# Softmax layers by pairs of heads on VectorE and ScalarE; the sparse layer's selection and splits in a new order

## The chip, the cores and the metric

The program runs on one core of a Trainium2 chip. The metric is device time in microseconds (us). The kernel before took 989.56 us (median of 3 runs, 987.58 to 989.96). Engines: PE is TensorE (PEld its weight loads), DVE VectorE, ACT ScalarE, POOL GpSimd, SP SyncE, which issues the weight loads from HBM.

## The reference

Two blocks run on 256 tokens of 1024 features, in fp32. The first has four layers: short convolution, sparse attention, latent attention, short convolution. The second has a pooling and a stick-breaking attention layer. The change touches the sparse and the latent layer.

```python
def dsa_mixer(xn, ...):      # sparse: 16 heads of 64, index 8 heads of 64
    q, k, v, z, qi, ki, wi = jnp.split(xn @ w_in, cuts, axis=-1)
    q = rope(rmsnorm(q, q_norm), positions); k = rope(rmsnorm(k, k_norm), positions)
    # score = sum over index heads of wi * relu(qi . ki), hidden keys masked
    # the 64 (seq // 4) largest scores of each query are kept
    # o = softmax(q k^T / 8 over the kept keys) v
    return (o * silu(z)) @ w_out

def mla_mixer(xn, ...):      # latent: 16 heads of 96 (64 + 32 rotary), v of 64
    cq, ckv, kr, z = jnp.split(xn @ w_in, cuts, axis=-1)
    q = (rmsnorm(cq, ..) @ w_uq); kv = (rmsnorm(ckv, ..) @ w_ukv)   # then norms, rope
    o = dense_chunk_attention(q, k, v, C_QK ** -0.5)
    return (o * silu(z)) @ w_out
```

## The kernel before

**Numbers in two parts.** Weights come in as fp32 (`raw`). ACT copies them to a shorter float (`whi`), DVE subtracts that from `raw` and leaves the low part (`wlo`). Activations are split alike (`xh`, `xl`, and `yh`, `yl` for gated outputs). `three` multiplies high by high, low by high and high by low, so a product costs three matmuls.

**Units.** Weights are streamed in units of 128 rows by 4096 columns, numbered B0, B0+1, ... for the sparse and C0, C0+1, ... for the latent layer. A unit stands in buffer u % 2 of `raw`, `whi` and `wlo`, so two are in flight. A split is done in halves of 2048 columns (`split`, DVE L883, ACT L470) or quarters of 1024 (`split_quarter`, DVE L902, ACT L478). In both loops of heads the out projection's last unit has its quarters' subtraction on POOL (L1581). Semaphores `landed`, `hi_ready`, `lo_ready`, `unit_done` connect SP, ACT, DVE and PE.

**Order.** Nothing schedules: each engine's instruction list is written out by hand, in the functions marked by engine, and an instruction waits on semaphores for its operands. So the order on each queue is the order of the code.

**Sparse layer.** B0 holds the index queries, B0+1 the index key and weights (`wi`), B0+2 to B0+5 the halves of q and k in turn (L396). For each of B0 and B0+2 to B0+5 (e = 0 to 4) ACT copies the accumulator (`token_raw`) and squares it (`token_squares`), DVE sums, DVE and ACT make the norm's factor (`half_mean`, `half_root`, `half_factor`), DVE and POOL apply norm and rotary (`token_turn`, `token_rope`), PE transposes (`turn_tokens`) and ACT or DVE copies the transposes (`token_out`). `index_scores` makes the eight heads' scores, ACT takes their relu, DVE sums them (`index_head`). `top64` selects: one pass that hides masked keys, then eight rounds of MAX (the 8 largest) and MATCH_REPLACE (which marks them), and a compare into `pick`. It is called for the first 128 queries (128 keys) and for the others (256 keys). B0+6 and B0+8 are the two halves of v, B0+7 and B0+9 those of z, B0+10 and B0+11 the out projection.

**Loops of heads.** `softmax_heads` runs on DVE and ACT for each layer. DVE reduces the logits of a head to a row minimum (L1171), ACT takes two exponentials (L669, L671), DVE divides by the sum (L1180, L1182), PE transposes, ACT copies the transposes (L678), PE multiplies with v, DVE multiplies by the gate (L1150). PE runs `paired_heads`: logits, transposes and products of two heads per step, between them one *filler* f: part of B0+8 or B0+9 (C0+7) or of the out projection (`attention_out`, a *piece*). ACT switches its function table for silu and back (`preload_act_table_set`). Behind the loop `attention_last_out` does the rest of the out projection. Before, DVE and ACT take one head a step (18 steps).

## Time and profile before

| | |
|---|---|
| runs | 989.56 us median, 987.58 to 989.96 |
| profiled execution | 994.89 us, its span 993.3 us, mean granted clock 0.97 |
| busy shares | PE 93%, PEld 87%, DVE 65%, ACT 50%, POOL 32% |
| sparse layer's token units, its loop, its rest | 131.2 to 235.2, to 308.1, to 325.4 us |
| latent layer's loop | 387.8 to 452.1 us |

The profile is of one execution. A granted clock of 1 is 2.4 GHz for TensorE, 0.5 is 1.2 GHz; a stretch's number is the mean over it. Idle time of an engine that PE does not wait for costs nothing.

### The profile page before, as it was taken

What the parts mean: (1) busy time and instruction counts of PE and PEld (TensorE: products, weight loads), DVE (VectorE), ACT (ScalarE), POOL (GpSimd) and SP (SyncE); (2) the same over time, 40 slices, a digit from 0 to 9 for tenths busy, and PEclk for the clock granted to TensorE, in tenths of its full rate; (3) what the DMA queues carried; (4) which work ended last, traced back from release to release, by engine and by line L of the source; (5) the groups of instructions that cost most, each with busy time, mean ns of one, the idle gap of its engine ahead of it and who ended that gap; (6) DMA issues with size and microseconds to landing.
All of it is one profiled execution on the core that took longest, in us unless ns stands there. A gap on an engine that the chain in (4) does not pass through costs nothing.

```text
span 993.3 us, 16780 instructions
## 1 busy us (share of the span) xinstructions
PE 924.2 (93%) x6761; PEld 865.9 (87%) x6761; DVE 643.1 (65%) x1005; ACT 500.3 (50%) x710; POOL 317.4 (32%) x270
## 2 busy tenths in 40 slices
PE   6999989988889996979999999899999999999986
PEld 5999978667668985869999999799999997988986
DVE  5776665895574788765576667587656554656642
ACT  5544454444574677673453352434445336575631
POOL 8433223343013225112543326955302000123320
PEclk9999999998889999799999999899999999999999
DMA  9876344434114425225477443344654562334401
GB/s 250 224 203 207 127 170 170 138 117 170 47 42 146 165 65 190 93 59 147 130 205 219 169 171 127 129 171 169 253 181 160 199 215 104 136 119 162 172 28 43
DMA packets 123585, 148.70 MB, mean 150 GB/s; under 512 B 9561, under 2 KB 79102, under 8 KB 123518
## 3 DMA queue, kind: packets, MB, share of 16 engines
q1 hardware_dynamic: 121472, 145.63, 45.3%
q0 software_dynamic: 464, 1.02, 0.4%
q10 hardware_dynamic: 1582, 1.12, 0.4%
q8 instruction: 47, 0.77, 0.3%
q14 instruction: 20, 0.16, 0.1%
HBM read 146.70 MB, written 1.05 MB: 149 GB/s over the span
## 4 chain that ended last, share of the span: by engine, by line
PE 61%; DVE 8%; ACT 7%; POOL 3%; issue 2%; ACTq 0%; DVEq 0%; POOLq 0%
PE acc L1652 43%; PE aux L1652 16%; DVE wlo L883 2%; POOL arena L1507 1%; POOL arena L1508 1%; ACT whi L478 1%; ACT arena L504 1%; ACT work L671 1%; POOL arena L1506 1%; ACT whi L470 1%; DVE score L1126 1%; PE aux L1996 1%; DVE arena L985 1%; DVE top L1125 1%; ACT work L678 1%
## 5 line engine op out<-in xcount | busy, mean ns | idle before, releaser
L883 DVE TENSOR_TENSOR wlo<-raw,whi 128x2048 fp32r<-128x2048 f32 (+5 forms) x118 | 281.0, 2408 | 104.9 <-ACT whi L470 103.1
L1652 PE MATMUL acc<-xh,whi 128*128 128x256 f32 x1128 | 323.9, 287 | 4.9 <-DVE wlo L883 4.2
L1652 PE MATMUL acc<-xl,whi 128*128 128x256 f32 x1128 | 321.1, 285 | 0.0
L1652 PE MATMUL acc<-xh,wlo 128*128 128x256 f32 x1128 | 321.0, 285 | 0.0
L470 ACT ACTIVATE whi<-raw 128x2048 fp32r<-128x2048 f32 (+5 forms) x118 | 202.9, 1748 | 85.1 <-PE aux L1652 44.0
L1652 PEld LDWEIGHTS acc<-xh,whi 128*128 128x128 f32 x1128 | 218.4, 194 | 6.8 <-issue 5.8
L1652 PEld LDWEIGHTS acc<-xl,whi 128*128 128x128 f32 x1128 | 218.3, 193 | 0.0
L1652 PEld LDWEIGHTS acc<-xh,wlo 128*128 128x128 f32 x1128 | 218.0, 193 | 0.0
L1652 PE MATMUL acc<-whi,xh 128*128 128x512 f32 (+1 forms) x208 | 83.4, 401 | 7.9 <-DVE arena L985 4.0
L1571 POOL CAST yh<-ytmp 128x256 fp32r<-128x256 f32 x24 | 17.0, 706 | 220.4 <-DVE ytmp L1409 123.3
L1652 PE MATMUL aux<-yh,whi 128*128 128x256 f32 x288 | 81.9, 284 | 0.0
L1652 PE MATMUL aux<-yh,wlo 128*128 128x256 f32 x288 | 81.5, 283 | 0.0
L1652 PE MATMUL aux<-yl,whi 128*128 128x256 f32 x288 | 81.5, 283 | 0.0
L1652 PE MATMUL acc<-whi,xl 128*128 128x512 f32 (+1 forms) x208 | 80.5, 387 | 0.0
L1652 PE MATMUL acc<-wlo,xh 128*128 128x512 f32 (+1 forms) x208 | 80.5, 387 | 0.0
L1652 PEld LDWEIGHTS acc<-whi,xh 128*128 128x128 f32 x208 | 40.2, 193 | 18.8 <-issue 6.5
L1652 PEld LDWEIGHTS aux<-yh,whi 128*128 128x128 f32 x288 | 55.3, 192 | 0.3 <-issue 0.3
L902 DVE TENSOR_TENSOR wlo<-raw,whi 128x1024 fp32r<-128x1024 f32 x44 | 53.9, 1225 | 2.2 <-ACT whi L478 2.2
L1652 PEld LDWEIGHTS aux<-yl,whi 128*128 128x128 f32 x288 | 55.3, 192 | 0.0
L1652 PEld LDWEIGHTS aux<-yh,wlo 128*128 128x128 f32 x288 | 55.3, 192 | 0.0
L1506 POOL TENSOR_TENSOR arena<-arena 128x1024 f32<-128x1024 f32 x5 | 12.1, 2412 | 124.5 <-ACT arena L504 124.5
L478 ACT ACTIVATE whi<-raw 128x1024 fp32r<-128x1024 f32 x48 | 50.1, 1046 | 0.0
(341 smaller groups left out, 1763.0 us busy)
## 6 DMA issues: line engine op xcount, KB each, us to landing
raw<-in_a_w_in SPq DMA_DIRECT2D x52, 512.0 KB, 6.6
raw<-in_sb_w_in SPq DMA_DIRECT2D x48, 512.0 KB, 5.5
raw<-in_b_w_in SPq DMA_DIRECT2D x36, 512.0 KB, 5.5
raw<-in_pool_w_in SPq DMA_DIRECT2D x32, 512.0 KB, 5.6
raw<-in_a_w_out SPq DMA_DIRECT2D x16, 512.0 KB, 5.0
raw<-in_pool_w_out SPq DMA_DIRECT2D x16, 512.0 KB, 5.0
raw<-in_sb_w_out SPq DMA_DIRECT2D x16, 512.0 KB, 4.9
raw<-in_b_w_out SPq DMA_DIRECT2D x8, 512.0 KB, 4.7
```

The costliest lines, as they stand in the source:

```text
L470: A(whi[b][:, lo:hi], (raw_third if third else raw[b])[:, lo:hi], ACT.Copy).then_inc(hi_ready, 1)
L478: ins = A(whi[u % 2][:, c * q:c * q + c], raw[u % 2][:, c * q:c * q + c], ACT.Copy)
L504: A(arena[:, 4 * n:4 * n + 4, :], xT[:, 4 * n:4 * n + 4, :], ACT.Square)\
L671: A(L[:, P:W384], L[:, P:W384], ACT.Exp, bias=st[:, 1:2], scale=nf[:, HEADS + i:HEADS + i + 1], accum_out=st[:, 3:4]).then_inc(sem("exp_re ...
L678: A(work[:, 2 + h % 2, :], aux[:, 2 + h % 2, 0:W384], ACT.Copy)\
L883: TT(wlo[b][:, lo:hi], (raw_third if third else raw[b])[:, lo:hi], whi[b][:, lo:hi].bitcast(F32), ALU.subtract).then_inc(lo_ready, 1)
L902: ins = TT(wlo[u % 2][:, c], raw[u % 2][:, c], whi[u % 2][:, c].bitcast(F32), ALU.subtract)
L985: ins = TT(dst, src, rb, ALU.mult)
L1125: me.link(V.max(top8[:, :], s))
L1506: me.link(TT(arena[:, 0:4, :], arena[:, 0:4, :], arena[:, 4:8, :], ALU.add))
L1571: nc.gpsimd.tensor_copy(hi, ytmp[:, :]).then_inc(sem("yh_ready"), 1)
L1652: return nc.tensor.matmul(out_, lhsT, rhs, start=start, stop=stop, skip_group_check=True)
```

## The change

- `softmax_heads` on DVE and ACT goes by pairs: two minima, the splits' quarters, two divisions (DVE); two heads' exponentials, two copies, two quarters (ACT), in eight steps and a tail.
- All quarters are subtracted on DVE, POOL's four of each loop go. The quarters' steps move; C0+7, which was split whole ahead of the latent loop, becomes quarters inside it, and is PE's filler 3, 5, 6, 8 there (before 5, 6, 8, 9). B0+9 is filler 5, 6, 8, 9 (before 6 to 9).
- Two more pieces of the out projection (half 1 of two tiles) become fillers 15 and 16, and `attention_last_out` has two fewer.
- `silu` of B0+7's z moves behind the first two heads' exponentials. The latent loop's turned heads 12 to 15 are spread over fillers 0 and 2.
- B0+2's first half is split in two quarters ahead of the layer's norm factor; the scores of the eight index heads stand in B0+3's steps 1 to 7 and B0+4's first, before in B0+4's eight; the token turns move one unit ahead.
- `top64` becomes `hide`, `take_largest(rounds)` and `chosen`: of the first 128 queries' eight rounds 3, 2 and 3 stand between the splits of B0+5, of the others' eight 3 ahead of B0+7's split and 5 behind it.

Lines that were removed, added or moved, with "..." where some are left out:

```diff
-        SPARSE_SPLITS = {first + q: (u, q) for first, u in ((2, B0 + 9), (8, B0 + 10), (12, B0 + 11)) for q in range(4)}
-        MLA_SPLITS = {first + q: (u, q) for first, u in ((2, C0 + 8), (11, C0 + 9)) for q in range(4)}
+        def quarters(u, halves):
+            return {step: tuple((u, 2 * half + n) for n in range(2)) for half, step in enumerate(halves)}
+        SPARSE_SPLITS = {**quarters(B0 + 9, (0, 1)), **quarters(B0 + 10, (3, 4)), **quarters(B0 + 11, (6, 7))}
+        MLA_SPLITS = {**quarters(C0 + 7, (0, 1)), **quarters(C0 + 8, (3, 4)), **quarters(C0 + 9, (6, 7))}
...
+            nc.scalar.preload_act_table_set("natural_log_exp_and_others")
             renorm(1, G_B)
             split(B0 + 1)
-            root(1)
-            nc.scalar.preload_act_table_set("natural_log_exp_and_others")
+            def first_half(u):
+                act.wait_ge(landed[u % 2], 64 * (u // 2))
+                act.wait_ge(unit_done, u - 1)
+                for q in range(2):
+                    c = slice(1024 * q, 1024 * q + 1024)
+                    A(whi[u % 2][:, c], raw[u % 2][:, c], ACT.Copy).then_inc(hi_ready if q else sem("quarter_hi"), 1)
+            first_half(B0 + 2)
+            root(1, log=True)
...
-            split(B0 + 2, (0,))
+            split(B0 + 2, (1,))
             act.wait_ge(sem("rt_ready"), 2)
             token_raw(0)
-            split(B0 + 2, (1,))
             act.wait_ge(unit_done, B0 + 2)
...
-            token_raw(1)
-            split(B0 + 4, (0,))
             act.wait_ge(sem("ki_turned"), 1)
             A(arena[:, 36, :], aux[:, 0, 0:T], ACT.Copy).then_inc(sem("ki_out"), 1)
             token_out(0)
-            token_squares(1)
-            split(B0 + 4, (1,))
-            token_raw(2)
+            token_raw(1)
             for h in range(8):
                 act.wait_ge(sem("idx_s"), h + 1)
...
                 if h == 1:
-                    split(B0 + 5, (0,))
-                if h == 3:
-                    token_squares(2)
-                if h == 5:
-                    split(B0 + 5, (1,))
+                    split(B0 + 4, (0,))
+                if h == 2:
+                    token_squares(1)
+                if h == 4:
+                    split(B0 + 4, (1,))
+            token_raw(2)
+            split(B0 + 5, (0,))
+            token_squares(2)
+            token_out(1)
+            split(B0 + 5, (1,))
             half_root(0)
             token_raw(3)
             split(B0 + 6, (0,))
             token_squares(3)
-            token_out(1)
+            token_out(2)
             split(B0 + 6, (1,))
             token_raw(4)
             split(B0 + 7, (0,))
             token_squares(4)
-            token_out(2)
             split(B0 + 7, (1,))
+            token_out(3)
             half_root(1)
-            token_out(3)
-            split(B0 + 8)
+            split(B0 + 8, (0,))
...
             values(vB, B0 + 6, 0, 0)
+            split(B0 + 8, (1,))
+            token_out(4)
...
-            silu(24, 4, 1)
             def softmax_heads(layer):
-                nc.scalar.preload_act_table_set("natural_log_exp_and_others")
                 h0 = HEADS * layer
                 y_count[0] += 8
-                for i in range(HEADS + 2):
-                    if layer == 0 and i == 4:
+                for j in range(HEADS // 2 + 1):
+                    for i in (2 * j, 2 * j + 1):
+                        if i < HEADS:
...
+                    if layer == 0 and j == 0:
+                        silu(24, 4, 1)
+                        nc.scalar.preload_act_table_set("natural_log_exp_and_others")
+                    if layer == 0 and j == 2:
                         values(vB, B0 + 8, 1, 1)
...
-                    if layer == 0 and i == 11:
-                        silu(28, 4, 2)
-                        nc.scalar.preload_act_table_set("natural_log_exp_and_others")
...
+                    if layer == 1 and j < 2:
+                        turn_copy(12 + 2 * j)
+                    if j:
+                        for h in (2 * j - 2, 2 * j - 1):
+                            act.wait_ge(sem("pt_psum"), h0 + h + 1)
+                            if h >= 2:
+                                act.wait_ge(sem("pv_done"), h0 + h - 1)
...
+                    for u, q in (SPARSE_SPLITS, MLA_SPLITS)[layer].get(j, ()):
+                        split_quarter(u, q)
+                    if j == 5:
+                        silu(44 if layer else 28, 4, 4 if layer else 2)
                         nc.scalar.preload_act_table_set("natural_log_exp_and_others")
...
+            def first_half(u):
+                for q in range(2):
+                    c = slice(1024 * q, 1024 * q + 1024)
+                    if q == 0:
+                        dve.wait_ge(sem("quarter_hi"), 1)
+                    else:
+                        dve.wait_ge(hi_ready, 2 * u + 1)
+                    TT(wlo[u % 2][:, c], raw[u % 2][:, c], whi[u % 2][:, c].bitcast(F32), ALU.subtract)\
+                        .then_inc(lo_ready if q else sem("quarter_lo"), 1)
+            mean_square(1)
+            first_half(B0 + 2)
...
+            newton(rT[:, 4:6], rT[:, 0:2], rT[:, 6:8]).then_inc(sem("rt_ready"), 1)
...
+            def hide(lo, hi):
                 s = score[:, lo:hi]
                 me.link(STT(s, mask[:, lo:hi], HIDDEN / NEG, s, ALU.mult, ALU.add))
-                for _ in range(TOPK // 8):
+            def take_largest(lo, hi, rounds):
+                s = score[:, lo:hi]
+                for _ in range(rounds):
...
-                TS(pick[:, lo:hi], s, (HIDDEN + TAKEN) / 2, NEG, ALU.is_gt, ALU.mult).then_inc(sem("picked"), 1)
+            def chosen(lo, hi):
+                TS(pick[:, lo:hi], score[:, lo:hi], (HIDDEN + TAKEN) / 2, NEG, ALU.is_gt, ALU.mult).then_inc(sem("picked"), 1)
+            for h in range(8):
+                index_head(h)
+                if h == 2:
+                    split(B0 + 4, (0,))
+                if h == 4:
+                    token_sums(1)
+                if h == 5:
+                    split(B0 + 4, (1,))
             dve.wait_ge(sem("mask_in"), 16)
-            top64(0, P)
+            hide(0, P)
+            take_largest(0, P, 3)
+            token_turn(2)
+            split(B0 + 5, (0,))
+            token_sums(2)
+            half_mean(0)
+            take_largest(0, P, 2)
+            half_factor(0)
+            split(B0 + 5, (1,))
+            take_largest(0, P, 3)
+            chosen(0, P)
+            token_turn(3)
             split(B0 + 6, (0,))
-            token_turn(3)
             token_sums(3)
             split(B0 + 6, (1,))
-            top64(P, W384)
+            hide(P, W384)
+            take_largest(P, W384, 3)
+            token_turn(4)
             split(B0 + 7, (0,))
-            token_turn(4)
             token_sums(4)
             half_mean(1)
             split(B0 + 7, (1,))
             half_factor(1)
+            take_largest(P, W384, 5)
+            chosen(P, W384)
             split(B0 + 8)
             take(B0 + 7, 24, "z_raw")
+            dve.wait_ge(sem("picked"), 2)
...
-            split(C0 + 7)
...
+                splits = (SPARSE_SPLITS, MLA_SPLITS)[layer]
+                def minima(i):
...
+                def division(h):
...
+                for j in range(HEADS // 2 + 2):
+                    if j == 5:
+                        take(C0 + 7 if layer else B0 + 9, 44 if layer else 28, "z_raw")
+                    if j < HEADS // 2:
+                        minima(2 * j)
+                        minima(2 * j + 1)
+                    if layer == 1 and j < 2:
+                        turn_copy(13 + 2 * j)
+                    if j >= 2:
+                        t = j - 2
...
+                    for n in range(2):
+                        if j - 1 in splits:
+                            split_quarter(*splits[j - 1][n])
+                        if j < HEADS // 2:
+                            division(2 * j + n)
...
-            def attention_low(u):
+            def attention_low():
                 for t in range(NK):
                     y_parts(yh[:, t, :], yl[:, t, :])
-                    if t in (4, 5):
...
-                        TT(wlo[u % 2][:, c], raw[u % 2][:, c], whi[u % 2][:, c].bitcast(F32), ALU.subtract)\
-                            .then_inc(lo_ready if t == 5 else sem("low_quarter"), 1)
...
+                    if u == B0 + 2 and k in (0, 2):
+                        pe.wait_ge(lo_ready if k else sem("quarter_lo"), 2 * u + 1 if k else 1)
+                    elif k in (0, 4):
...
+            def index_first(k):
+                if k:
+                    index_scores(k - 1)
+            def index_last(k):
+                if k == 0:
+                    index_scores(7)
+                if k == 3:
+                    turn_tokens(1)
...
-            token_unit(B0 + 3, ki_turn)
+            token_unit(B0 + 3, index_first)
             taken("tok_raw", 4)
-            token_unit(B0 + 4, index_scores)
+            token_unit(B0 + 4, index_last)
             taken("tok_raw", 6)
-            token_unit(B0 + 5, turn_at({2: 1}))
+            token_unit(B0 + 5, turn_at({5: 2}))
             taken("tok_raw", 8)
-            token_unit(B0 + 6, turn_at({4: 2}))
+            token_unit(B0 + 6, turn_at({4: 3}))
             taken("tok_raw", 10)
-            unit(B0 + 7, in_tiles(1), xh, xl, turn_at({4: 3}))
+            unit(B0 + 7, in_tiles(1), xh, xl, turn_at({6: 4}))
...
-                if 6 <= f < 10:
-                    if f == 6:
+                if f in (5, 6, 8, 9):
+                    if f == 5:
                         taken("v_ready", 4)
-                    unit(B0 + 9, in_tiles(1), xh, xl, part=(2 * (f - 6), 2))
-                if f in (12, 13, 15, 16):
-                    if f == 12:
-                        taken("z_raw", 2)
-                    attention_out(B0 + 10, 8, (12, 13, 15, 16).index(f), 0)
+                    unit(B0 + 9, in_tiles(1), xh, xl, part=(2 * (5, 6, 8, 9).index(f), 2))
+                out_filler(f, 0)
+            def out_filler(f, layer):
+                u, y0 = (C0 + 8, 16) if layer else (B0 + 10, 8)
+                if f == 11:
+                    taken("z_raw", 2 * layer + 2)
+                if 11 <= f < 15:
+                    attention_out(u, y0, f - 11, 0)
+                if 15 <= f < 17:
+                    if f == 15:
+                        taken("logits", HEADS * layer + HEADS)
+                    attention_out(u, y0, f - 15, 1)
...
-                if f < 2:
-                    turn_heads(12 + 2 * f)
-                    turn_heads(13 + 2 * f)
-                if f in (5, 6, 8, 9):
-                    if f == 5:
-                        taken("turn_out_v", 7)
+                if f in (0, 2):
+                    turn_heads(12 + f)
+                    turn_heads(13 + f)
+                if f in (3, 5, 6, 8):
+                    if f == 3:
+                        taken("turn_out_v", 8)
                         taken("turn_out_a", 8)
-                    unit(C0 + 7, in_tiles(1), xh, xl, part=(2 * (5, 6, 8, 9).index(f), 2))
-                if f in (12, 13, 15, 16):
-                    if f == 12:
-                        taken("z_raw", 4)
-                    attention_out(C0 + 8, 16, (12, 13, 15, 16).index(f), 0)
+                    unit(C0 + 7, in_tiles(1), xh, xl, part=(2 * (3, 5, 6, 8).index(f), 2))
+                out_filler(f, 1)
...
-                for k in range(4):
+                for k in range(2, 4):
```

**DVE, ahead of B0+7's split.** In the rows below `raw_50`, `whi_52` and `wlo_54` are the buffers of odd units, `raw_49`, `whi_51`, `wlo_53` those of even ones. Before:

```order
L1125 MAX top_115<-score 128x8
L1126 MATCH_REPLACE score<-top_115,score 128x256
L1127 TENSOR_SCALAR pick<-score 128x256
L883 TENSOR_TENSOR wlo_54<-raw_50,whi_52 128x2048
L1054 TENSOR_TENSOR sqy<-sqy,qk_tab 128x8x32
L1055 TENSOR_TENSOR sqy<-sqy,qk_tab 128x8x32
```

The same place in the changed kernel:

```order
L1145 MAX top_115<-score 128x8
L1146 MATCH_REPLACE score<-top_115,score 128x256
L1082 TENSOR_TENSOR sqy<-sqy,qk_tab 128x8x32
L1083 TENSOR_TENSOR sqy<-sqy,qk_tab 128x8x32
L1082 TENSOR_TENSOR sqy<-sqy,qk_tab 128x8x32
L1083 TENSOR_TENSOR sqy<-sqy,qk_tab 128x8x32
L892 TENSOR_TENSOR wlo_54<-raw_50,whi_52 128x2048
L1091 TENSOR_REDUCE hf<-sqy 128x8 x2
L1096 TENSOR_SCALAR hf<-hf 128x4x8
L892 TENSOR_TENSOR wlo_54<-raw_50,whi_52 128x2048
```

Before, the eighth round and the pick stand right ahead of the first half. Now the third round does, with the last token turn between; five rounds and the pick follow the second half.

**ACT, start of the sparse loop.** L646 (L659) writes v, L653 (L668) is silu, L586 (L600) a copy of transposes. Before:

```order
L470 ACTIVATE whi_51<-raw_49 128x2048 x2
L646 ACTIVATE vB<-acc,rT 128x512 x2
L653 ACT_TABLE_LOAD
L653 ACTIVATE arena<-arena 128x1024
L658 ACT_TABLE_LOAD
L669 ACTIVATE work,stat<-work,stat,nf 128x128
L671 ACTIVATE work,stat<-work,stat,nf 128x256
L669 ACTIVATE work,stat<-work,stat,nf 128x128
L671 ACTIVATE work,stat<-work,stat,nf 128x256
L586 ACTIVATE arena<-acc 128x4x128 x2
```

After:

```order
L474 ACTIVATE whi_51<-raw_49 128x2048
L659 ACTIVATE vB<-acc,rT 128x512 x2
L474 ACTIVATE whi_51<-raw_49 128x2048
L600 ACTIVATE arena<-aux 128x4x128 x2
L679 ACTIVATE work,stat<-work,stat,nf 128x128
L681 ACTIVATE work,stat<-work,stat,nf 128x256
L679 ACTIVATE work,stat<-work,stat,nf 128x128
L681 ACTIVATE work,stat<-work,stat,nf 128x256
L668 ACT_TABLE_LOAD
L668 ACTIVATE arena<-arena 128x1024
L685 ACT_TABLE_LOAD
L482 ACTIVATE whi_52<-raw_50 128x1024 x2
```

The values stand between B0+8's halves, and silu with its two table loads behind the first two heads.

**ACT, start of the latent loop.** L709 (L719) copies turned heads. Before:

```order
L709 ACTIVATE arena<-acc,G 96x512
L470 ACTIVATE whi_52<-raw_50 128x2048 x2
L658 ACT_TABLE_LOAD
L669 ACTIVATE work,stat<-work,stat,nf 128x128
L671 ACTIVATE work,stat<-work,stat,nf 128x256
L709 ACTIVATE arena<-acc,G 96x512
```

After:

```order
L719 ACTIVATE arena<-acc,G 96x512
L679 ACTIVATE work,stat<-work,stat,nf 128x128
L681 ACTIVATE work,stat<-work,stat,nf 128x256
L679 ACTIVATE work,stat<-work,stat,nf 128x128
L681 ACTIVATE work,stat<-work,stat,nf 128x256
L719 ACTIVATE arena<-acc,G 96x512
L482 ACTIVATE whi_52<-raw_50 128x1024 x2
```

C0+7's split (two halves of 2048) is gone from ahead of the exponentials and follows as quarters.

## Rows read from the trace of the kernel before

**Rows 1.** The page's first part: each engine's busy time.

```profile
PE 924.2 (93%) x6761; PEld 865.9 (87%) x6761; DVE 643.1 (65%) x1005; ACT 500.3 (50%) x710; POOL 317.4 (32%) x270
```

**Rows 2.** Stretches: us, busy PE, PEld, DVE, ACT, POOL, clock, DMA, GB/s.

```profile
131.20:235.20 104.00, 96.58 (x486) 78.71 (x484) 77.92 (x141) 53.31 (x70) 42.87 (x36) 0.97 0.43 151
235.20:308.10 72.90, 59.73 (x378) 47.74 (x377) 43.20 (x150) 44.85 (x102) 10.82 (x15) 0.84 0.22 77
308.10:325.40 17.30, 17.30 (x147) 17.24 (x144) 7.01 (x10) 5.27 (x8) 2.99 (x5) 1.00 0.57 193
387.80:452.10 64.30, 51.31 (x337) 42.19 (x336) 47.07 (x153) 42.01 (x97) 13.30 (x18) 0.87 0.23 67
```

**Rows 3.** PEld's timeline: start, us, instruction, [idle before, releaser].

```profile
148.75 0.19 PEld L1652 LDWEIGHTS acc<-whi,xh 128*128 128x128 f32 x1 [3.48 <-issue]
...
221.53 0.29 PEld L1652 LDWEIGHTS acc<-xh,whi 128*128 128x128 f32 x1 [4.56 <-issue]
...
238.79 0.29 PEld L1652 LDWEIGHTS acc<-whi,xh 128*128 128x128 f32 x1 [2.92 <-DVE arena L985]
...
397.06 0.66 PEld L1953 LDWEIGHTS acc<-cst,qraw 128*96 128x96 f32 x4 [6.53 <-ACT arena L709]
```

**Rows 4.** Stretches at either clock, columns as in rows 2.

```profile
131.10:141.90 10.80, 10.80 (x50) 8.97 (x49) 6.16 (x7) 4.76 (x7) 6.61 (x12) 1.00 0.37 123
273.10:281.40 8.30, 8.30 (x72) 7.47 (x70) 3.65 (x17) 4.22 (x12) 1.13 (x2) 1.00 0.29 118
411.00:416.90 5.90, 5.90 (x48) 5.20 (x48) 4.49 (x18) 1.58 (x5) 1.13 (x2) 1.00 0.01 3
221.50:228.50 7.00, 6.94 (x47) 6.97 (x48) 6.74 (x13) 0.46 (x2) 2.74 (x2) 0.79 0.02 1
238.70:247.00 8.30, 8.21 (x24) 6.48 (x24) 2.18 (x14) 4.57 (x10) 0.00 (x0) 0.63 0.64 248
```

**Rows 5.** ACT's timeline ahead of B0+2.

```profile
144.39 1.91 ACT L470 ACTIVATE whi<-raw 128x2048 fp32r<-128x2048 f32 x1
146.21 1.25 ACT L571 ACTIVATE sqy<-acc,rT 128x512 f32<-128x512 f32 x2
```

**Rows 6.** DVE's timeline at the selection's end and at B0+8.

```profile
211.05 0.43 DVE L1125 MAX8 top<-score 128x8 f32<-128x256 f32 x1
...
219.13 2.28 DVE L883 TENSOR_TENSOR wlo<-raw,whi 128x2048 fp32r<-128x2048 f32 x1
...
232.19 5.34 DVE L883 TENSOR_TENSOR wlo<-raw,whi 128x2048 fp32r<-128x2048 f32 x2 [3.78 <-ACT whi L470]
```

**Rows 7.** DVE's timeline: one head of the sparse loop.

```profile
263.03 0.28 DVE L1171 CUSTOM_DVE_ANT_0 work<-aux,pick 128x128 f32<-128x128 f32 x1
...
263.78 0.16 DVE L1180 RECIPROCAL stat<-stat 128x2 f32<-128x2 f32 x1
...
264.44 1.22 DVE L902 TENSOR_TENSOR wlo<-raw,whi 128x1024 fp32r<-128x1024 f32 x1
```

**Rows 8.** ACT's timeline: one head of the sparse loop.

```profile
291.91 1.28 ACT L684 ACT_TABLE_LOAD   x1
293.21 0.49 ACT L669 ACTIVATE work<-work,stat,nf 128x128 f32<-128x128 f32 x1
...
294.29 0.47 ACT L678 ACTIVATE work<-aux 128x384 f32<-128x384 f32 x1
294.66 1.04 ACT L478 ACTIVATE whi<-raw 128x1024 fp32r<-128x1024 f32 x1
```

**Rows 9.** ACT's groups, 235.2 to 308.1: busy, mean ns, idle before.

```profile
L646 ACT ACTIVATE vB<-acc,rT 128x512 f32<-128x512 f32 x2 | 1.3, 684 | 0.0
```

**Rows 10.** ACT's timeline, start of the latent loop.

```profile
396.34 0.67 ACT L709 ACTIVATE arena<-acc,G 96x512 f32<-96x512 f32 x1
```

**Rows 11.** Timelines of DVE and of POOL, end of the latent loop.

```profile
447.19 3.03 DVE L1182 TENSOR_SCALAR work<-work,stat 128x128 f32<-128x128 f32 x2
...
447.70 2.37 POOL L1581 TENSOR_TENSOR wlo<-raw,whi 128x1024 fp32r<-128x1024 f32 x1
```

127 lines of the change are left out of this document (37 added, 90 removed).

## The prediction

> **What bounds the kernel now.** I read the page first: TensorE (PE) is busy 93% of the span [rows 1], so the change can only win where PE waits or runs at its low clock. Then the table of stretches over the layers that the diff touches [rows 2]. The reader is to see four things in it. In the token projections (131.2 to 235.2) PE is busy 96.6 of 104.0 us. In the sparse layer's softmax loop (235.2 to 308.1) it is busy 59.7 of 72.9 us, and the granted clock is 0.84. In the output part behind it (308.1 to 325.4) it never waits: 144 matmuls in 17.3 us, 0.12 each. In the latent layer's loop (387.8 to 452.1) it is busy 51.3 of 64.3 us at clock 0.87. Then PE's timeline shows where the long waits are [rows 3]: 3.5 us ahead of unit B0+2, 4.6 ahead of B0+7, 2.9 ahead of B0+8, and 6.5 in the latent layer, where the turned heads wait for ScalarE (ACT). Last, stretches at either clock give the prices [rows 4]: B0's 48 matmuls of 512 columns take 10.8 us (0.225 each) at 2.4 GHz, but 24 of them take 8.2 (0.34) behind the 2.9 us wait; B0+7's first 47 of 256 columns take 7.0 instead of 5.6 behind the 4.6 us wait. A wait of 3 to 5 us thus costs another 1.3 to 2.7 us of low clock.
>
> Two undisturbed stretches give the cost of one pair of heads. 273.1 to 281.4 holds a pair and 48 filler matmuls (5.8 us), so the pair costs 2.5; 411.0 to 416.9 holds a pair of the latent layer and 24 fillers (2.9), so 3.0.
>
> **Start of B0+2.** PE needs the two accumulator copies of B0 (token_raw) and the first low part. Before, ACT does a half split (1.9), then the copies, which start at 146.21 and end at 147.5 [rows 5]; VectorE (DVE) then subtracts until 148.6. Now ACT does two quarters from 142.1, two small logarithm steps, the other half, then the copies: 142.1 + 1.9 + 0.5 + 1.9 + 1.1 = 147.6. DVE's first quarters are ready by 145.4. So the copies end it and not the split: 1.1 us gained of 3.5. Bounds: nothing, and 3.5 plus the low clock behind it, 1.5. I take 1.1, since every term of it is a copy whose row exists. The table switches that the diff takes away here lie ahead of the copies.
>
> **Index scores and turns moved.** The eight index steps keep their number and their switches of array shape; they only start seven steps earlier. Token turns 0 and 1 move ahead of B0+5, 2 to 4 each one unit ahead; five are then done when the loop begins, instead of four. That puts one turn, 1.0 us, ahead of the loop and takes it out of it. Nothing queued behind them becomes late by my walk: relu h is 0.5 us, and DVE's step with a split behind it ends before the next but one.
>
> **The selection's rounds spread.** Eight rounds on 256 columns and a pick of 0.2 stand between 211.05 and 219.13 [rows 6], 0.98 a round. They are one piece ahead of B0+7's first half (219.13, 2.28 us), which PE waits for until 221.5. Now three rounds stand ahead of it and five behind its second half. The half moves 5 rounds earlier against its surroundings (4.9 us), and PE's need does not move: B0+6 ends near 217.4, the half is ready near 214.8, the second near 218.4 against a need of 223. The wait of 4.6 and the low clock's 1.3 go. What is late next is B0+8: the rounds end near 224.6, both halves near 229.1, and `take` (1.2) waits for B0+7's end near 229.9. The walk's slack is 2.6, 4.6 and 0.8 us; if DVE were 1 us later throughout, only the last would cost. Before, that place was held by ACT, which came to B0+8 late: DVE idled 3.8 us for it [rows 6].
>
> Sum to the loop's start: 1.1 + 4.6 + 1.3 - 1.0 (the fifth turn) = 6.0 us.
>
> **The sparse loop.** Before: 8 pairs 20.0, B0+8 10.8, B0+9's 96 matmuls 11.5, four output pieces 5.8, one turn 1.0: 49.1 us of work in 72.9, so 23.8 lost. Now two more output pieces (half 1, 24 matmuls, 2.9 us) fill it, and the turn is gone: 51.0. For the waits I walked the four queues pair by pair. Prices: minima 0.75 and division 0.66 a head, a quarter 1.14 on DVE [rows 7]; exponentials 1.08 a head on ACT (293.21 to 294.29), a copy 0.4 and a quarter 1.0 [rows 8], so DVE's fullest step is 2 x (0.75 + 0.66 + 1.14) + 0.4 for the gate = 5.5 us and ACT's 2 x (1.08 + 0.4 + 1.0) = 5.0, against 5.4 to 8.3 on PE with two fillers. Because each split quarter now stands between a minimum and the division that waits for ACT, DVE has something to do in that gap. Waits that remain: 0.9 for B0+7's `take`; 2.7 at filler 5, where the second value half comes behind two minima, two heads' exponentials and 1.3 us of copies [rows 9] (0.75 + 2.2 + 1.3 + 0.2 = 4.4 after the logits, of which PE fills 1.7), with 1.5 of low clock behind it; 0.9 at the last pair. That is 6.0. For waits too short for such a walk I add 0.5 a pair, 4.0. Loop: 61.0, gain 11.9 us. Bounds: 0 (every wait only moves) and 21.9 (none is left). Behind the loop 24 matmuls fewer: 2.9 us, sure, since that stretch has no waits [rows 2].
>
> **The latent loop.** Before: 8 x 3.0, C0+7 11.5, four pieces 5.8, four turned heads 1.8: 43.1 of 64.3, 21.2 lost. The 6.5 us wait came from C0+7's whole split ahead of the loop: two halves of 2.28 on DVE [rows 6], and ACT's turn copy (0.67) only after the first exponentials, at 396.34 [rows 10]. Now the loop starts at once, but C0+7 becomes filler 3, and its first two quarters come late on DVE: four minima 3.0, two turn copies 1.4 (like ACT's), three divisions 2.0, five small factor steps of 0.2 each, like the reciprocal, 1.0, two quarters 2.3: 9.8 us after the first logits, while PE has 4.7 of work. So 5.2 us of that wait come back, with 2.5 of low clock, and 0.9 at the end: 8.6, and 4.0 as above. 46.0 + 8.6 + 4.0 = 58.6, gain 5.7. Bounds: 0 and 18.3. Again 2.9 behind the loop.
>
> **POOL gives up its four low quarters.** While it did them, two divisions on DVE (0.66 a pair normally) took 3.0 us [rows 11]. DVE pays 1.14 for each instead. The gain is inside the walk (the last pairs).
>
> The SBUF page of the Trainium skill ("SBUF — State Buffer", Who interferes with whom) says that a VectorE operation with two SBUF inputs and a GpSimd operation that reads SBUF exclude one another for the whole instruction. It makes a rival, below.
>
> ACT's table loads take 1.28 us and the exponential starts 0.02 later [rows 8]; the loops keep six of them. The Trainium skill ("ScalarE: Activation LUTs", What ACT_TABLE_LOAD costs) gives 2.66 us for a switch, with a drain behind the load. By that the two switches at step 5 of each loop would delay the exponentials by 2.8 us more, and the sum would be near 966; by the row there is no drain here, and I leave it out.
>
> **Sum.** 6.0 + 11.9 + 2.9 + 5.7 + 2.9 = 29.4 us. The profiled execution took 994.89 (span 993.3), so it would take 965.5; the median of the runs is 989.56, 5.3 lower, and I take the same difference off it: 960.2 us.
>
> **Rivals.**
> (a) The pairs hand over one at a time: ACT's copies wait for transposes behind a filler, and its splits stand behind the copies, so PE waits once a pair. For it: in the old latent loop PE waited 6.5 us for one copy of ACT that stood behind other work [rows 3, 10]. Against: PE's fillers last longer than either chain. Half of the loops' gain goes: 8.8 us, 969.
> (b) The exclusion above: the last token's product on GpSimd (rope) now ends near 224.1, DVE's B0+8 split begins near 224.6. If GpSimd is 0.5 us late, two subtractions of 2.28 [rows 6] pass ahead of it, PE waits some 2.5 us in B0+7 and runs low behind it: 5 us, 965. For it: [rows 11] show one engine stretched beside the other. Against: the slack, though small.
> (c) Slower: PE's short waits in both loops keep it at 1.2 GHz. Its work there, 97 us, costs 1.5 times as much at that level [rows 4], 48.5 us. It eats the gain from 60% of the loops' work on; at four fifths it costs 38.8, and the time is 970 + 29 = 999. Against: the clock of the old loops is 0.84 and 0.87, with more waits.
> (d) Next to nothing left: filler 3 and filler 5 find their operands in time: 950.
> (e) The change does not reach the path: the same time. Only if every removed wait reappears; the 5.8 us of output work moved into waits speak against it.
>
> **Numbers.** The forecast 0.70 (own range 952 to 968), (a) 0.13, (b) 0.05, (c) 0.04, (d) 0.05, (e) 0.03. Range 948 to 975. 0.3%, 3 us, is about what a measurement of this kernel can tell from no change: faster 0.93, same 0.03, slower 0.04.
>
> **What would show it.** No wait ahead of B0+7; B0+2 starting 2.3 to 2.5 us after B0+1; B0+8 starting 7 to 9 us earlier; loop B 58 to 64 us and loop C 56 to 62; one wait of about 3 us at filler 5 and one of about 5 ahead of C0+7; 120 matmuls in 14.4 us behind each loop; no DVE division of 3 us. I am wrong if the loops take over 68 and 62 us, or if their clock falls under 0.8.

## The result and the profile after

The changed kernel takes 965.67 us (median of 4 runs, 965.41 to 966.42) against 989.55 (987.58 to 989.96). The ratio is 0.9747, with a 95% interval of 0.972 to 0.9775, so it is 23.9 us faster. The forecast was 960.2, with a range of 948 to 975. One run of the kernel before, beside the experiments, took 1132.9 us at a clock of 0.749 and is left out of every comparison.

Its profiled execution took 965.70, with a span of 964.1. I read the page's first part first, as in [rows 1].

```profile
PE 907.5 (94%) x6761; PEld 853.6 (89%) x6761; DVE 651.7 (68%) x1011; ACT 498.3 (52%) x712; POOL 322.0 (33%) x266
```

PE's instructions are as many as before, yet it is busy 16.7 us less. Nothing was taken out of its work; the same matmuls ran at a higher clock. The table of stretches, with the columns of [rows 2], shows where: the token units, the sparse loop, its tail, the latent loop and its tail.

```profile
131.80:234.70 102.90, 95.64 (x495) 77.09 (x493) 83.81 (x141) 52.53 (x71) 45.02 (x36) 1.00 0.44 152
234.70:294.50 59.80, 53.20 (x393) 43.88 (x392) 45.41 (x152) 43.81 (x100) 12.59 (x14) 0.97 0.27 94
294.50:309.10 14.60, 14.60 (x124) 14.49 (x121) 7.33 (x11) 5.28 (x8) 1.14 (x2) 1.00 0.71 234
371.40:427.00 55.60, 47.77 (x361) 41.45 (x360) 45.77 (x157) 40.46 (x98) 13.27 (x16) 0.97 0.25 76
427.00:441.50 14.50, 14.50 (x123) 14.36 (x120) 8.87 (x11) 6.34 (x8) 1.13 (x2) 1.00 0.76 206
```

The granted clock of the loops rose from 0.84 and 0.87 [rows 2] to 0.97 in both. The next table sets the stages of the two traces side by side. Their bounds are read from PE's timeline: the end of the layer before, the first logits, the last product with v, and the last matmul of the out projection. They add up within 0.1 us, by rounding.

| stage | before | after | gain | forecast |
|---|---|---|---|---|
| start of B0 | 131.2 | 131.9 | -0.7 | 0 |
| B0 to the sparse loop | 104.2 | 102.8 | 1.4 | 6.0 |
| sparse loop | 72.6 | 59.7 | 12.9 | 11.9 |
| its tail | 17.5 | 14.6 | 2.9 | 2.9 |
| up to the latent loop | 62.4 | 62.4 | 0 | 0 |
| latent loop | 64.1 | 55.5 | 8.6 | 5.7 |
| its tail | 17.5 | 14.6 | 2.9 | 2.9 |
| the rest | 523.8 | 522.5 | 1.3 | 0 |
| span | 993.3 | 964.1 | 29.2 | 29.4 |

The sum came out and the stages did not: the token units gave 4.6 us less than forecast, the two loops 3.9 more and the rest 0.6 more. That the sum fits is luck. PE's timeline after, with the columns of [rows 3], has the waits:

```profile
148.43 0.19 PEld L1693 LDWEIGHTS acc<-whi,xh 128*128 128x128 f32 x1 [2.48 <-ACT sqy L585]
...
202.93 0.20 PEld L1860 LDWEIGHTS aux<-cst,sqy 128*128 128x128 f32 x2 [3.06 <-POOL sqy L1608]
...
208.17 0.19 PEld L1693 LDWEIGHTS acc<-whi,xh 128*128 128x128 f32 x1 [0.88 <-issue]
...
221.80 0.19 PEld L1693 LDWEIGHTS acc<-xh,whi 128*128 128x128 f32 x1 [1.99 <-issue]
...
237.04 0.19 PEld L1693 LDWEIGHTS acc<-whi,xh 128*128 128x128 f32 x1 [1.80 <-DVE arena L994]
...
255.19 0.19 PEld L1693 LDWEIGHTS acc<-xh,whi 128*128 128x128 f32 x1 [2.99 <-ACT vB L659]
...
382.78 0.29 PEld L1693 LDWEIGHTS acc<-xh,whi 128*128 128x128 f32 x1 [5.34 <-issue]
```

These are the starts of B0+2, token 2's transposes (in B0+5), B0+6, B0+7, B0+8, B0+9 (filler 5) and C0+7. Ahead of B0+2 and B0+7 the waits shrank from 3.48 and 4.56 [rows 3] to 2.48 and 1.99. The 3.06 and the 0.88 are new. Filler 5 and C0+7 wait as forecast (2.7 and 5.2).

### The profile page after: what moved, and what is told of

Its sections match the earlier page's. It is cut to its first block, busy times and chain, and to the rows that moved or that the text cites. A ratio compares the mean times of both kernels' runs of the same rounds, so it can differ in the third digit from the quotient of the medians.

```text
span 964.1 us, 16784 instructions
## 1 busy us (share of the span) xinstructions
PE 907.5 (94%) x6761; PEld 853.6 (89%) x6761; DVE 651.7 (68%) x1011; ACT 498.3 (52%) x712; POOL 322.0 (33%) x266
## 4 chain that ended last, share of the span: by engine, by line
PE 60%; DVE 10%; ACT 6%; POOL 3%; issue 2%; ACTq 0%; POOLq 0%; DVEq 0%
PE acc L1693 43%; PE aux L1693 16%; DVE wlo L892 3%; POOL arena L1553 1%; ACT work L681 1%; POOL arena L1554 1%; ACT arena L508 1%; POOL arena L1552 1%; ACT work L679 1%; DVE arena L994 1%; DVE score L1146 1%; ACT work L695 1%; DVE sqy L1083 1%; DVE top L1145 1%; DVE work L1209 0%
## 5 line engine op out<-in xcount | busy, mean ns | idle before, releaser
L892 DVE TENSOR_TENSOR wlo<-raw,whi 128x2048 fp32r<-128x2048 f32 (+5 forms) x115 | 276.6, 2432 | 85.7 <-ACT whi L474 83.9
L474 ACT ACTIVATE whi<-raw 128x2048 fp32r<-128x2048 f32 (+5 forms) x115 | 197.3, 1744 | 78.6 <-PE acc L1693 38.1
L1617 POOL CAST yh<-ytmp 128x256 fp32r<-128x256 f32 x24 | 24.3, 1011 | 216.9 <-DVE ytmp L1455 123.3
L911 DVE TENSOR_TENSOR wlo<-raw,whi 128x1024 fp32r<-128x1024 f32 x52 | 64.8, 1250 | 2.0 <-ACT whi L482 1.9
L482 ACT ACTIVATE whi<-raw 128x1024 fp32r<-128x1024 f32 x52 | 53.1, 1048 | 0.0
```

The costliest lines, as they stand in the source:

```text
L474: A(whi[b][:, lo:hi], (raw_third if third else raw[b])[:, lo:hi], ACT.Copy).then_inc(hi_ready, 1)
L482: ins = A(whi[u % 2][:, c * q:c * q + c], raw[u % 2][:, c * q:c * q + c], ACT.Copy)
L892: TT(wlo[b][:, lo:hi], (raw_third if third else raw[b])[:, lo:hi], whi[b][:, lo:hi].bitcast(F32), ALU.subtract).then_inc(lo_ready, 1)
L911: ins = TT(wlo[u % 2][:, c], raw[u % 2][:, c], whi[u % 2][:, c].bitcast(F32), ALU.subtract)
L1617: nc.gpsimd.tensor_copy(hi, ytmp[:, :]).then_inc(sem("yh_ready"), 1)
```

## What stretched in the token units

The wait of 3.06 us is for GpSimd's last product of token 2. POOL's timeline has its two products of that kind, and DVE's timeline two splits and a rotary product in the same stretches:

```profile
195.90 2.95 POOL L1608 TENSOR_TENSOR sqy<-sqy,hf 128x512 f32<-128x512 f32 x1 [6.10 <-DVE nf L1105]
...
201.78 1.10 POOL L1608 TENSOR_TENSOR sqy<-sqy,hf 128x512 f32<-128x512 f32 x1
```

```profile
187.13 1.53 DVE L1083 TENSOR_TENSOR sqy<-sqy,qk_tab 128x256 f32<-128x256 f32 x1
188.58 3.37 DVE L892 TENSOR_TENSOR wlo<-raw,whi 128x2048 fp32r<-128x2048 f32 x1
...
218.32 3.37 DVE L892 TENSOR_TENSOR wlo<-raw,whi 128x2048 fp32r<-128x2048 f32 x1
```

The same product takes 2.95 us beside a split and 1.10 alone. A half split takes 3.37 instead of 2.28 [rows 6], and 218.32 is the half of B0+7 that PE waits for. On the way to token 2's transposes, the rotary product (1.53 instead of 0.42), the split behind it and GpSimd's product come one after the other, and together they take 4.1 us more than alone. That is an estimate from these rows; by it the stretching is enough for the whole wait of 3.06.

This is the exclusion that rival (b) spoke of, in other places. The rule of the Trainium skill ("SBUF — State Buffer", Who interferes with whom), that a VectorE operation with two SBUF inputs and a GpSimd operation that reads SBUF keep each other out, agrees with these rows: the product that starts at 195.90 ends at 198.85, 0.9 us behind the split that began at 195.67 and took 2.28.

## The experiments

The changed kernel was timed once, in the 4 runs above. Before's median beside the later groups of runs was 989.62 (for the first four experiments), 989.97 (the next four) and 991.15 (the last four), so a difference of 1 to 2 us from 965.67 is no more than these groups differ by themselves. A ratio is to before's runs of the same group, with its 95% interval.

Theory: the loops gain by the pairs' order, in place; in the token units PE asks for token 2 earlier than GpSimd can have it, and the splits beside the rotary work are stretched. Rivals: the loops' gain is low clock of one traced execution; VectorE's own queue limits the token units.

**The kernel before once more, traced.** No edit.

> The kernel before, once more with a profile. Its profiled execution took 994.89 us, 5.3 over the median of 989.55, and I had taken that 5.3 as an offset that the changed kernel would have too; it did not (profiled 965.70, median 965.67). Theory: the excess is low clock in the two softmax loops that most executions don't have, so this execution comes to 987 to 990 and its loops are 2 to 5 us shorter than 72.8 and 64.3. Rival: being profiled costs this kernel 5 us; then it takes 994 to 996 with the same loops.

It took 997.70 us. The two loops are as long as in the first trace, to 0.1 us, by PE's timeline; the bounds here are rounded (columns of [rows 2]):

```profile
235.50:308.30 72.80, 59.68 (x378) 47.75 (x376) 43.12 (x150) 44.75 (x102) 10.69 (x15) 0.84 0.22 77
388.00:452.30 64.30, 49.84 (x337) 40.97 (x336) 47.05 (x153) 41.99 (x97) 13.27 (x18) 0.89 0.23 67
```

My forecast for this execution failed, and the loops did not get shorter. The rival asked for 994 to 996 with the same loops, which is nearer, but it is not shown either. Of 29 timed runs of this kernel, 24 took 986.8 to 991.5 us, at a clock of 0.977 to 0.979 in the 20 that have it recorded, and five took 994.9 to 998.5, four of them at 0.969 to 0.970. The two traced ones (994.9 at 0.970, 997.7 at 0.967) belong to the upper group, and the upper group comes without tracing too. The changed kernel's 4 runs have none like it (965.4 to 966.4, at 0.985 to 0.991), but 4 are few to tell. For the other kernels the traced execution is one of the timed runs; it is the slowest of `short_rope` (959.97) and the fastest of `values_early` (963.26), so tracing has no fixed price. In which stage before's 5 us arise, and whether tracing brings them on there, stays open, since no trace of a run near 989 exists.

**The latent loop alone,** on the kernel before.

In short:

```diff
-            split(C0 + 7)
+MLA_SPLITS = {C0+7: steps 0, 1; C0+8: 3, 4; C0+9: 6, 7}; layer 1 takes the new softmax_heads and fillers
```

> The kernel before with the latent loop of the changed one alone (pairs, C0+7's quarters inside, quarters on VectorE, two pieces of the out projection inside). In the two profiles the loop and its tail are 8.6 + 2.9 = 11.5 us shorter. Theory: each part's gain is its own, less a share of the 5.3 us: 978 to 981. Rival: the loop's gain was the low clock of that one execution, and only the 2.9 us of work moved and the 1 us net of its first wait are left: 985 to 987.

982.92 us (980.48 to 984.79), ratio 0.9912 (0.9862 to 0.9962): 6.7 us, and by the interval 4 to 14. Its trace has the loop at 56.8 and the tail at 14.6, so 10.2 us less than in before's trace. The result lies between the two expectations, so part of the traced gain probably belongs to before's slower executions.

**Both loops,** on the kernel before.

In short:

```diff
+for j in range(HEADS // 2 + 1): ...   # both layers by pairs
+                    if layer == 0 and j == 1:
+                        token_out(4)     # the fifth turn stays in the loop, as before
```

> The kernel before with both loops of the changed one; the token units, the selection and B0+2 stay as before. Theory, from the two profiles: the token part gave 1.3 us of the 6.0 that I forecast, so the loops alone make 966.5 to 968.5. Rival, by my forecast: the token part is worth 6.0 and hides in the total, 971 to 973. A third: the token part costs time by itself, and this is below 965.

971.37 us (971.00 to 974.79), ratio 0.9832 (0.98 to 0.9864). The sparse loop is thus worth 982.92 - 971.37 = 11.5 us, and the token part, with B0+8's order, 971.37 - 965.67 = 5.7. That is the rival's number, but not by its way: between the two traces the token units are 2.8 us shorter (105.6 to 102.8), the sparse loop 1.3 (61.0 to 59.7), and the latent loop, whose code is the same, 1.4 (56.9 to 55.5).

**GpSimd's rotary work cut** (`short_rope`). The rotary is left out for tokens 2 to 4 and the norm's factor reaches one head of eight.

```diff
-                me.link(TT(raw, raw, over_heads(cos), ALU.mult))
-                ins = TT(raw, raw, turn, ALU.add)
+                if e > 1:
+                    cut = slice(0, 8)
+                    me.link(TT(raw[:, 0:1, cut], raw[:, 0:1, cut], turn[:, 0:1, cut], ALU.add))
+                    ins = TT(raw[:, 0:1, cut], raw[:, 0:1, cut], turn[:, 0:1, cut], ALU.add)
...
```

> The changed kernel with GpSimd's rotary products of q and k cut to 8 elements each for B0+3 to B0+5's tokens (the rotary and the norm's factor are left out there). Theory: PE's new wait of 3.06 us in B0+5 is for GpSimd's last product of token 2, and the waits of 0.88 and 1.99 ahead of B0+6 and B0+7 come from VectorE operations stretched beside GpSimd's (3.37 us instead of 2.28, 1.5 instead of 0.42); all three go, 960 to 961, and no VectorE half split in 186 to 222 us takes over 2.4 us. Rival: VectorE's own queue (rounds, turns, splits) sets these waits; then PE's waits move to B0+6 and the time stays at 964 to 966, though the stretched ones are gone.

958.72 us (957.99 to 959.97), ratio 0.9692 (0.9668 to 0.9715), 7.0 us under the changed kernel. One stretch of each trace, of the changed kernel:

```profile
188.00:229.50 41.50, 36.59 (x197) 30.76 (x196) 39.36 (x69) 20.09 (x25) 23.50 (x15) 1.00 0.39 136
```

and of this one, with two of its splits from DVE's timeline:

```profile
188.00:229.50 41.50, 41.50 (x242) 36.62 (x240) 37.95 (x78) 22.31 (x27) 7.93 (x16) 1.00 0.52 182
```

```profile
188.54 2.28 DVE L892 TENSOR_TENSOR wlo<-raw,whi 128x2048 fp32r<-128x2048 f32 x1
...
210.97 2.29 DVE L892 TENSOR_TENSOR wlo<-raw,whi 128x2048 fp32r<-128x2048 f32 x1
```

PE is busy all of 41.5 us instead of 36.6, and all six half splits there take 2.28 or 2.29. VectorE's instructions and their order are the same, so its queue was not the limit. Of PE's waits of 3.06, 0.88 and 1.99 none is left, and the one ahead of B0+8 fell from 1.80 to 0.93: 6.8 us, against 7.0 by the timed runs. The cut shortens GpSimd's work as well as the overlap, so it doesn't part the two.

**Splits ahead of the turns.**

```diff
-            token_turn(3)
             split(B0 + 6, (0,))
-            token_sums(3)
-            split(B0 + 6, (1,))
             hide(P, W384)
-            take_largest(P, W384, 3)
-            token_turn(4)
+            take_largest(P, W384, 1)
+            token_turn(3)
+            token_sums(3)
+            split(B0 + 6, (1,))
+            take_largest(P, W384, 2)
             split(B0 + 7, (0,))
+            token_turn(4)
...
-            token_unit(B0 + 5, turn_at({5: 2}))
-            token_unit(B0 + 6, turn_at({4: 3}))
-            unit(B0 + 7, in_tiles(1), xh, xl, turn_at({6: 4}))
+            token_unit(B0 + 5)
+            token_unit(B0 + 6, turn_at({3: 2}))
+            unit(B0 + 7, in_tiles(1), xh, xl, turn_at({2: 3, 6: 4}))
```

On ScalarE, the second half of B0+6 also moves ahead of the copy of token 2's transposes.

> The changed kernel; on VectorE both halves of B0+6 and the first of B0+7 stand ahead of token turns 3 and 4, with part of the second block's rounds between, and PE turns token 2 in B0+6 and token 3 in B0+7 instead of one unit earlier. Theory: PE's waits of 3.06, 0.88 and 1.99 us come from the place of the rotary work beside VectorE's splits; in this order PE asks later and the first halves run while GpSimd is idle: 3 to 5 us less, 961 to 963. Rival: VectorE and GpSimd get the same work in the same stretch, and the stretched operations only change places; the waits reappear ahead of B0+7 and B0+8: 964 to 966.

961.62 us (961.34 to 962.82), ratio 0.9711 (0.9671 to 0.9751), 4.05 less: within the theory's range. PE's waits between 188 and 231 us, by its timeline:

```profile
210.52 0.19 PEld L1694 LDWEIGHTS acc<-whi,xh 128*128 128x128 f32 x1 [1.20 <-DVE wlo L892]
...
227.16 0.42 PEld L1861 LDWEIGHTS aux<-cst,sqy 128*128 128x128 f32 x4 [1.22 <-POOL sqy L1609]
```

5.93 us of waits (3.06, 0.88, 1.99) became 2.42. GpSimd is stretched still (a 1.34 us operation takes 3.39 at 199.86), but PE asks for its result six steps of k later.

**The second values one step earlier** (`values_early`).

```diff
-                    if layer == 0 and j == 2:
-                        values(vB, B0 + 8, 1, 1)
...
+                    if layer == 0 and j == 1:      # behind the quarters
+                        values(vB, B0 + 8, 1, 1)
```

> The changed kernel with ScalarE's copies of B0+8's values (1.25 us) one step earlier, behind step 1's quarters instead of step 2's exponentials. Theory: PE's wait of 2.98 us at filler 5 is for these copies; ScalarE is free from 250.3 to 251.7, so the wait falls under 1 us and the low clock behind it (24 matmuls in 4.26 us instead of 2.93) goes: 962 to 963.5. Rival: PE then waits at filler 5 for the next pair's products or B0+9's low quarters instead, and the time stays within 1 us of 965.7.

963.76 us (963.26 to 966.88), ratio 0.974 (0.9697 to 0.9782), 1.9 less. Its runs overlap the changed kernel's and were taken in another group, so the gain of the whole is not clear of noise; the trace shows the wait gone. ScalarE copies at 250.94 now, and PE goes into filler 5 without a wait; the sparse loop is 55.2 us in this trace instead of 59.7.

```profile
250.94 1.25 ACT L659 ACTIVATE vB<-acc,rT 128x512 f32<-128x512 f32 x2
252.32 0.49 ACT L679 ACTIVATE work<-work,stat,nf 128x128 f32<-128x128 f32 x1
```

But the latent loop, unchanged, is 56.8 instead of 55.5, and the token units 104.4 instead of 102.8. Of the 4.5 us in the sparse loop, 3.0 are the wait and 1.3 the low clock behind it, and the next stretches show that low clock is not this edit's alone to give. Behind the wait ahead of B0+2, which is 2.48 and 2.47 us and has the same code, the changed kernel's trace is at full clock and this one is not:

```profile
148.40:151.20 2.80, 2.77 (x12) 2.33 (x13) 2.75 (x6) 2.05 (x2) 0.95 (x2) 1.00 0.24 18
```

```profile
147.40:151.40 4.00, 3.94 (x11) 3.16 (x12) 3.95 (x6) 2.07 (x3) 2.12 (x2) 0.63 0.40 97
```

**`take` between the halves of B0+8.**

```diff
-            split(B0 + 8)
+            split(B0 + 8, (0,))
             take(B0 + 7, 24, "z_raw")
...
+                    if layer == 0 and j == 0:      # behind the first two minima
+                        split(B0 + 8, (1,))
```

> The changed kernel with VectorE's second half of B0+8 behind the first two minima of the sparse loop, so that B0+7's `take` comes 2.2 us earlier. Theory: the wait of 1.81 us ahead of B0+8 goes: 963.5 to 964.5. Rival: the second half becomes the late one at filler 2, or the first divisions wait, and the time does not move by more than 0.5 us.

966.22 us (964.79 to 968.12): no gain, as the rival had it, though not for its reason. The wait fell from 1.80 to 0.93 and the sparse loop to 57.4, of which 1.3 us is that no low clock followed filler 5's wait (24 matmuls in 2.92 us instead of 4.26). But the latent loop with the same code took 57.2.

**C0+7's quarters ahead of the minima.**

```diff
+                    if layer == 1 and j == 1:
+                        for n in range(2):
+                            split_quarter(*splits[0][n])
                     if j < HEADS // 2:
                         minima(2 * j)
```

> The changed kernel with C0+7's first two quarters on VectorE ahead of the second pair's minima in the latent loop. Theory: they end 2.8 us earlier, and PE's wait of 5.34 us ahead of C0+7 shrinks by that, with some low clock behind it (24 matmuls in 4.38 us instead of 2.93): 961.5 to 963. Rival: the second pair's exponentials and divisions come 2.4 us later and PE waits for them instead: 965 to 967.

967.56 us (967.41 to 968.60), 1.9 more, with the same doubt as to noise; the wait ahead of C0+7 grew from 5.34 to 6.91. Both expectations missed the cause. PE's row for C0+7, the two quarters on VectorE and turn copy 14 on ScalarE:

```profile
383.87 0.28 PEld L1697 LDWEIGHTS acc<-xh,whi 128*128 128x128 f32 x1 [6.91 <-issue]
```

```profile
377.85 2.36 DVE L911 TENSOR_TENSOR wlo<-raw,whi 128x1024 fp32r<-128x1024 f32 x2 [0.87 <-ACT whi L482]
```

```profile
383.13 0.67 ACT L719 ACTIVATE arena<-acc,G 96x512 f32<-96x512 f32 x1
```

The quarters were done at 380.2. The filler also waits for the turn copies 14 and 15, and copy 14 stands on ScalarE behind exponentials that wait for the minima which were put back. It ends at 383.8, and PE starts at 383.87. Copy 15, on VectorE behind the minima, had ended at 382.4, so it was copy 14 that decided.

**Two edits together** (splits ahead of turns, values earlier), **and a third,** with the turn copies moved too.

```diff
+                    if layer == 1 and j == 1:     # VectorE, ahead of the minima
+                        turn_copy(15)
+                        for n in range(2):
+                            split_quarter(*splits[0][n])
...
+                    if layer == 1 and j == 1:     # ScalarE, ahead of the exponentials
+                        turn_copy(14)
```

> The changed kernel with the two edits that helped alone (splits ahead of turns: 4.05 us less; the second values one step earlier: 1.9 less). Theory: they act in different places and add up, 959 to 960.5. Rival: the low clock that one of them saves turns up elsewhere, as where the latent loop, with the same code, took 55.5 to 57.2 us in five traces: 961 to 962.

> As two_fixes, and in the latent loop C0+7's first two quarters stand ahead of the second pair's minima, behind the turn copies 14 and 15, which are moved ahead too. Quarters ahead of minima alone had made PE wait 6.91 us instead of 5.34, since the filler waits for turn copy 15 as well. Theory: with both ahead the wait falls to 3 to 3.5 us, and the time is 2 to 3 us under two_fixes: 956.5 to 958.5. Rival: the second pair's divisions come late instead, within 0.7 us of two_fixes.

Two: 959.35 us (957.98 to 960.62), 6.3 less than the changed kernel, where 4.05 + 1.9 = 6.0 was the sum. Three: 957.08 us (955.01 to 959.22), ratio to before 0.9649 (0.9618 to 0.968). The wait ahead of C0+7 was 4.70 in the trace of two, and with the third it is

```profile
374.35 0.29 PEld L1701 LDWEIGHTS acc<-xh,whi 128*128 128x128 f32 x1 [3.29 <-issue]
```

as expected. The gain over two is 2.3 us by the medians, but the runs of the two overlap (957.98 to 960.62 and 955.01 to 959.22), so its size is uncertain. The shorter wait is shown. This is the fastest version: 34.1 us under the runs of before beside it (991.15) and 8.6 under the changed kernel.

**GpSimd's quarters back.** These are two in each loop, four in all, as many as the kernel before had there.

```diff
+                    if t in (4, 5):
+                        TT(wlo[..], raw[..], whi[..], ALU.subtract)   # GpSimd, between the gated outputs
...
-                        if j - 1 in splits:
+                        if j - 1 in splits and j - 1 < 7:
```

> The changed kernel with the last two quarters of each loop's last unit back on GpSimd, as before. Theory (my forecast's step): while GpSimd does one, VectorE's divisions take 3.0 us instead of 0.66 a pair, so PE waits in the last two steps of each loop; 1 to 3 us more than 965.7: 967 to 969. Rival: in the last steps VectorE has nothing else late, and the quarters cost the same either way: 965 to 966.5.

974.10 us (973.36 to 974.60), 8.4 more. No division takes 3 us now: the longest in the loops are 1.1, as in the changed kernel, and none stands beside a quarter. The cost came by another way. The quarters stand in GpSimd's list between two gated outputs. Its timeline, VectorE's and PE's at the end of the sparse loop:

```profile
291.36 2.36 POOL L1629 TENSOR_TENSOR wlo<-raw,whi 128x1024 fp32r<-128x1024 f32 x1 [7.95 <-ACT whi L482]
293.66 0.40 POOL L1619 CAST yh<-ytmp 128x256 fp32r<-128x256 f32 x1
```

```profile
294.99 0.42 DVE L1194 TENSOR_TENSOR ytmp<-acc,arena 128x256 f32<-128x256 f32 x1 [4.77 <-POOL yl L1509]
```

```profile
295.53 0.44 PEld L1700 LDWEIGHTS acc<-work,vB 128*64 128x64 f32 x6 [3.17 <-issue]
```

GpSimd waits for ScalarE's high part, splits, and only then makes the gated output; VectorE's gate waits 4.8 us for it, and PE 3.2 for the gate. The loops take 62.2 and 59.4 us instead of 59.7 and 55.5, and the tails are 1.4 and 0.9 longer.

**The moved pieces back behind the loops.**

```diff
-                if 15 <= f < 17: ...
-                    attention_out(u, y0, f - 15, 1)
...
-                for k in range(2, 4):
+                for k in range(4):
```

> The changed kernel with the two moved pieces of each out projection back behind the loop. Theory: the two loops' last steps have waits that the pieces fill, so each tail is 2.9 us longer and each loop less than that shorter: by PE's waits at the last pairs, 1 to 2 us a loop are lost, 967.5 to 970. Rival: the pieces fill no wait but stand in the chain, and the time stays within 1 us of 965.7.

970.71 us (969.16 to 971.03), 5.0 more. The loops are only 1.1 and 0.1 us shorter without them (58.6 and 55.4), and the tails 2.9 longer each. The second of these is blurred, since this trace began the latent loop at the low clock (8 loads in 2.25 us instead of 1.18). By the timed runs the waits at the end of the loops hid 5.0 of the 5.8 us of work. I had expected them to hide about half.

## Why the prediction came out as it did

**The offset failed.** Against the traced execution the sum was 29.4 and the traces show 29.2. The step that missed is the last one: "I take the same difference off it". The 5.3 us between before's traced execution and its median was no offset of every kernel: the changed kernel's traced execution is 0.03 us from its median. Without it the forecast would have been 965.5, and that would have hit by luck, since the stages' errors cancel.

**Which stages fell short depends on what one compares with.** By the traces the part ahead of the sparse loop is short of the forecast and the loops are over it. By the timed runs the change is worth 23.9 us: the loops with their tails gave 6.7 and 11.5, where the forecast had 8.6 and 14.8, and the rest gave 5.7 where it had 6.0. Before's 5 us, which no trace near its median shows, lie between the two views. So the waits below are shown, and the stages' shares in the time are not.

**Start of B0+2: right.** Forecast 1.1 us, and the wait named ScalarE's copy, as said; it is 1.0 shorter (3.48 to 2.48). In this trace the low clock behind it went too, which I had kept only as a bound: the first 12 matmuls take 2.58 us instead of 4.17. The table in the last section shows it back in five of the ten traces with this wait. (The terms of the copies' end add to 147.5, not 147.6.)

**Token turns one unit ahead: wrong.** "Nothing queued behind them becomes late by my walk" is the step. Token 2's transposes can only follow GpSimd's last product, which waits for the norm's factor; I had priced one side of the move, PE's 1.0, and walked VectorE and ScalarE at their undisturbed durations. GpSimd's product of 2.95 us beside a split, and the stretched rotary product and split ahead of it, make PE wait 3.06.

**The selection's rounds: half right.** The wait of 4.56 ahead of B0+7 fell to 1.99, and not to nothing, since its half split took 3.37 and the turn ahead of it 1.1 more than alone; By my walk that half was ready near 214.8; it was ready at 221.7, and at 213.3 in the run with GpSimd's work cut, so what the walk left out is GpSimd: token turn 3 alone holds VectorE from 200.16 to 205.77, and there it takes 1.4. One of its rows is stretched and waits for GpSimd's product:

```profile
202.98 1.42 DVE L1082 TENSOR_TENSOR sqy<-sqy,qk_tab 128x256 f32<-128x256 f32 x1 [1.00 <-POOL sqy L1608]
```

VectorE came to `take` late too, with 1.80 us of wait where I had 0.8 of slack. So B0+8 starts 1.8 us earlier, not 7 to 9. Rival (b) had the mechanism, with the wrong token and 0.05; the run with GpSimd's work cut prices it at 7.0 us in all, the stretching and the length of the work together. Rival (b)'s 965 is the measured time, but only by way of the offset that failed.

**The sparse loop: right, in part by luck.** 61.0 forecast, 59.7 measured. At filler 5 I had 2.7 us of wait and 1.5 of low clock; it is 2.99, and 24 matmuls take 4.26 instead of 2.93. Moving the copies took the wait away, so its cause is shown. The low clock behind it is there in only half of the traces with this wait.

**The latent loop: mechanism right, size off.** C0+7 waits 5.34 (forecast 5.2), with 1.4 of low clock behind it and not 2.5 (the traces with this wait have 1.4 to 2.3). For short waits I had 4.9 in all, and about 2.8 are left (55.5 - 46.0 - 5.3 - 1.4). (My terms up to the quarters' end add to 9.7, not 9.8.) What I did not see is that C0+7 waits for ScalarE's turn copy as well, which ends at 381.2, only 1.5 us ahead of the quarters. That took back the gain when the quarters alone were moved.

**GpSimd's quarters: right to be taken off, wrong price.** I looked at the stretched divisions [rows 11]; the row is the two operations of one head's division, which take 0.55 alone, and not of two. In the new order the price is the gated outputs behind the quarters in GpSimd's list, 8.4 us.

**The other rivals.** (c) fell with the clock of 0.97 in both loops, (a) with the loops' gain of 21.5 us in the traces, and 12.4 by the timed runs (18.2 less 5.8 for the tails), where it allowed 8.8, (e) with the time, and (d) since both waits that it did without are there. The forecast's other sum, near 966 with a drain behind ScalarE's table loads, comes close to the time by accident: in the changed kernel's trace a load starts at 278.54, takes 1.28, and the silu starts at 279.84, so there is no drain.

## What to carry to other kernels

When a step is moved earlier on the engine that needs it, walk every engine that makes its operand, GpSimd too, with the durations that its work has beside the others. List all semaphores that a waiting piece takes, not only the one that came last: with the late operand moved ahead, the next one decides. A traced execution may sit off the median for one kernel and not for the next, so look at the spread of the timed runs before taking an offset from them. A wait can be priced from a row; whether low clock follows it cannot be told from one trace.
